# First RMSNorm of a hybrid encoder step: squares added in pairs by DVE, half of them made later on ACT

## The chip, the cores and the metric

The kernel runs on one core of a Trainium2 chip. The metric is the device time of one execution in microseconds. A core has TensorE (PE, with the weight loads shown as PEld), VectorE (DVE), ScalarE (ACT), GpSimd (POOL) and SyncE (SP, which here only issues DMAs), each with its own queue of instructions, run in order. They meet only through semaphores.

## The reference

Two layers of a streaming encoder over 544 tokens (512 of a prompt, 32 of a running stream), model width 1024:

```python
def rmsnorm(x, g):
    x32 = x.astype(jnp.float32)
    y = x32 * lax.rsqrt(jnp.mean(x32 * x32, axis=-1, keepdims=True) + EPS)
    return (y * g.astype(jnp.float32)).astype(x.dtype)

def swiglu(h, wg, wu, wd):
    return (jax.nn.silu(h @ wg) * (h @ wu)) @ wd

# per layer
x = x + 0.5 * swiglu(rmsnorm(x, norm_ffn1), w_gate, w_up, w_down)
x = x + merge(gla(z), band_attention(z)) @ w_out        # z = rmsnorm(x, norm_mix) @ w_in
x = x + 0.5 * swiglu(rmsnorm(x, norm_ffn2), w_gate, w_up, w_down)
# at the end one more rmsnorm
```

There are seven norms. The change concerns the first alone, ahead of layer 0's first FFN.

## The kernel before, in words

**Layout.** Activations lie transposed: `x` is [128 partitions, 8 tiles, 544 tokens], tile k holding features 128k to 128k+127. A norm over features is therefore a sum over partitions and over the eight tiles. The kernel never normalises before a product. It multiplies the weights with x times gain, and scales the products afterwards by S, the inverse root of the mean square of each token. So the sum of squares is wanted only when the first products are there.

**Precision.** Weights and activations are each split into a high part in fp32r (made by ACT, a Copy) and a low part (made by DVE, a subtraction); a product is three fp32r matmuls over 272 tokens, half of the 544.

**Gate and up product.** For each pair of column tiles there is a block of seven products of half size (`a11`, `a12`, `s1`, `s2`, `s4`, `s3`, `a22`), each with four k-tiles, so 84 matmuls a block. They use four PSUM banks; `s2` goes to the bank of `a11`, `s4` to that of `s1`, `s3` again to that of `s2`. TensorE waits (`after_copy` in `block`, L744) until ACT has copied the product that was there (`copy_out`, L1100 to L1104). Block 0 has an order of its own, `FIRST_ORDER`: three k-tiles of `a11`, of `a12` and of `s1`, then the fourth of each, three of `s2`, three of `a22`, the fourth of `s2`, all of `s4` and of `s3`, and the last of `a22`. Between `s3` and that last k-tile of `a22` stands `stats` of the norm.

**Statistics.** `stats(norm)` (L691, its matmul is L700) multiplies a 128x128 matrix of ones with tiles of squares, in plain fp32, once for each half of the tokens, accumulating in PSUM. For all later norms DVE has added the squares up and two tiles are left. For the first norm (`norm == 0`) it takes the eight tiles `first_squares` directly, each when `sq_made` says that it is there. Then ACT takes the square root (`rms_of`, L1033, which needs a table load) and DVE the reciprocal (L1398). Block 1's `s1` on TensorE waits for `rms_ready`, since its bank held the sums.

**Squares of the first norm.** ACT makes them with `first_square(k)` (L1199), into `ev`, `tk`, `tmp`, `sil` and `sq_tmp`, all of them free at this time. The order of ACT's start is written out by hand at L1201 to L1222: splits of tokens and weights as they arrive, squares 0 to 3 between them, then `v_split(0)` (L1060), `t_split(0, 3)` (L1098), `q_split(0)` (L1072), the squares 4 to 7, and then `ffn(0)`. There the function `block` of ACT (L1119) copies `a11`, splits block 1's weights (`x_split`, L1051), copies `s1`, copies `s2`, goes on to `v_split` and `y_split` (L1066) of block 1, the root, the copy of `a22` and `q_split`.

**DVE's start** is written out as well (L1595 to L1615): sums and low parts, ending with `v_split(0)` (L1427), `t_split(0, 3)` (L1474), `q_split(0)` (L1431). Its function `block` (L1506) makes the low part of the next block's weights (`x_split`, L1418), the two adds of `v_sums` (L1440, L1442) and `quads(b, 0)` (L1484), then `v_split`, `y_split` (L1422) and `quads(b, 1)`.

**Loads.** SP issues a raw tile for block b+2 (L490) when DVE has made both the low part and `v_sums` of block b, and its side tile (L498) after `y_split` of block b. POOL adds a second tile to the side tile by an accumulating DMA (L570).

Of the kernel before, what the change touches and what calls it, by code (L numbers as in the profile page):

```python
# [28 lines left out]
ACT = mybir.ActivationFunctionType  # L29
# [10 lines left out]
KT = D_MODEL // P  # L40
# [99 lines left out]
def x_sum(norm, pos):  # L140

    layer, n = divmod(norm - 1, 3)
    return layer * X_SUMS + (DOWN_UNITS - KT, DOWN_UNITS, X_SUMS - KT)[n] + pos + 1
# [46 lines left out]
def encoder_step(nc, xT, bias_rev, vectors,  # L190
# [3 lines left out]
    with ctx:  # L194
        def sb(name, shape, dt=f32, scope=ctx):
            return scope.enter_context(nc.sbuf_tensor(name, shape, dt))

        def sem(name):
            return ctx.enter_context(nc.semaphore(name))


        x = sb("x", [P, KT, T])
# [6 lines left out]
        sq_acc = sb("sq_acc", [P, T])  # L209
        sq_tmp = sb("sq_tmp", [P, T])  # L210
        tmp = sb("tmp", [P, 2, T])
        sil = sb("sil", [P, T])
# [57 lines left out]
        first_squares = [ev[:, 1, n, :] for n in range(2)] + [tk[:, 1, n, :, :].rearrange("p a b -> p (a b)") for n in range(2)]  # L270
# [19 lines left out]
        def block_banks(b):  # L290

            f, i = b // BLOCKS, b % BLOCKS // 2
            return sides(f, sum(i >= i0 for i0, _ in GROUPS) - 1)[b % 2]

        def sums_in(norm):

            layer, n = divmod(norm, 3)
            if n == 1 or norm == 3 * DEPTH:
                return [px[0][:, a, 0:HALF] for a in range(2)]
            return [half[:, 1, 0:HALF] for half in sides(2 * layer + n // 2, 0)[1]]  # L300
# [17 lines left out]

        x_loaded = [sem(f"x_loaded{k}") for k in range(KT)]
        sq_made = sem("sq_made")  # L320
        vec_loaded = sem("vec_loaded")
        ext_loaded = sem("ext_loaded")
        ext_stored = sem("ext_stored")
# [104 lines left out]
        def product(b, p):  # L428

            return len(PRODUCTS) * b + PRODUCTS.index(p) + 1  # L430
# [233 lines left out]
        def _(pe):  # L664
# [26 lines left out]
            def stats(norm):  # L691

                if norm:
                    pe.wait_ge(sq_step, norm * SQ_ADDS)
                squares = [sq_acc[:, :], sil[:, :]] if norm else first_squares
                for a in range(2):
                    for n, sq in enumerate(squares):
                        if a == 0 and sq is not squares[0] or norm == 0:
                            pe.wait_ge(sq_made, KT + norm if norm else n + 1)
                        mm = pe.matmul(sums_in(norm)[a], ones[:, :], sq[:, a * HALF:(a + 1) * HALF],  # L700
                                       start=(n == 0), stop=(n == len(squares) - 1))
                mm.then_inc(stats_done, 1)
# [99 lines left out]
            for layer in range(0, DEPTH):  # L802
# [3 lines left out]
                norm = 3 * layer + 1  # L806
# [210 lines left out]
        def _(act):  # L1017
# [12 lines left out]
            def rms_of(norm):  # L1030
                act.wait_ge(stats_done, norm + 1)
                for a, sums in enumerate(sums_in(norm)):
                    act.activation(S[:, a * HALF:(a + 1) * HALF], sums, ACT.Sqrt, bias=eps[:, :],  # L1033
                                   scale=1.0 / D_MODEL).then_inc(rms_ready, 1)

            def square(norm, n, m):

                act.wait_ge(x_summed, x_sum(norm, n))
                if n >= 3:
                    act.wait_ge(sq_step, (norm - 1) * SQ_ADDS + n - 2)  # L1040
                dst = sq_acc if n == 0 else sil if n % 2 else sq_tmp
                act.activation(dst[:, :], x[:, m, :], ACT.Square).then_inc(sq_made if n == KT - 1 else sq_tile, 1)
# [57 lines left out]
            def copy_out(b, p, dst):  # L1100
                bc, ad = block_banks(b)
                src = {"A": ad[:, 0, 0:HALF], "C": bc[:, 1, 0:HALF], "D": ad[:, 1, 0:HALF]}[BANK[p]]
                act.wait_ge(prod_done, product(b, p))
                act.activation(dst, src, ACT.Copy, scale=-1.0 if p == "s1" else 1.0).then_inc(taken, 1)  # L1104
# [14 lines left out]
            def block(b, begins, after):  # L1119

                part = tk[:, b % 2, :, :, :]
                if b >= 2:
                    act.wait_ge(quad_made, 2 * (b - 2) + 2)
                copy_out(b, "a11", part[:, 0, 0, :])
                if after is not None:
                    x_split(after)
                else:
                    run_split(b, 0)
                copy_out(b, "s1", part[:, 1, 1, :])
                copy_out(b, "s2", part[:, 0, 1, :])  # L1130
                if not begins:
                    block_end(b - 1)
                if after is not None:
                    v_split(after)
                    y_split(after)
                else:
                    run_split(b, 1)
                if b % BLOCKS == 0:
                    rms_of(b // BLOCKS // 2 * 3 + b // BLOCKS % 2 * 2)
                copy_out(b, "a22", part[:, 1, 0, :])  # L1140
                if after is not None:
                    q_split(after)
                else:
                    run_split(b, 2)
                    block_end(b)
# [49 lines left out]

            act.wait_ge(vec_loaded, 16)
            gain = lambda m: g1[:, m:m + 1]
            def first_square(k):
                act.activation(first_squares[k], x[:, k, :], ACT.Square).then_inc(sq_made, 1)  # L1199

            stage(0, 0, gain)  # L1201
            stage(0, 1, gain)
            b_split(0, 0)
# [14 lines left out]
            v_split(0)  # L1218
            t_split(0, 3)
            q_split(0)  # L1220
            for k in range(4, KT):
                first_square(k)  # L1222
            act.wait_ge(const_made, 11)
            for layer in range(0, DEPTH):
                ffn(2 * layer)
# [127 lines left out]
                b = first_block(f, 0)  # L1353
# [28 lines left out]
        def _(dve):  # L1382
# [18 lines left out]
            def square_sum(norm, n):  # L1401
# [3 lines left out]
                    dve.wait_ge(sq_step, (norm - 1) * SQ_ADDS + n - 1)  # L1405
                dve.tensor_tensor(sq_acc[:, :], sq_acc[:, :], (sil if n % 2 else sq_tmp)[:, :], ALU.add).then_inc(sq_step, 1)

            def pair_sums(norm, n):

                if n in (2, 4, 6):  # L1410
                    if n > 2:
                        square_sum(norm, n - 2)
                    square_sum(norm, n - 1)
# [15 lines left out]
            def q_split(b):  # L1429
                dve.wait_ge(q_hi, b + 1)  # L1430
                dve.tensor_tensor(ql[:, :], raw_q[b % 2][:, :], qh[:, :].bitcast(f32), ALU.subtract).then_inc(q_lo, 1)  # L1431

            def v_sums(b):

                n = RAW_POS["block", b]
                raw_there(dve, ("block", b))
                dve.wait_ge(y_summed[b % 2], 16 * (b // 2 + 1))
                if b:
                    dve.wait_ge(v_lo, b)
                dve.tensor_tensor(raw_v[:, 0:SUB], raw_y[b % 2][:, 1, :], raw[n % 2][:, 0:SUB], ALU.add).then_inc(v_part, 1)  # L1440
                dve.wait_ge(v_part, b + 1)
                dve.tensor_tensor(raw_v[:, SUB:2 * SUB], raw_v[:, 0:SUB], raw[n % 2][:, SUB:2 * SUB],  # L1442
                                  ALU.add).then_inc(v_made, 1)
# [33 lines left out]
            def quads(b, half):  # L1477

                bc, ad = block_banks(b)
                part = tk[:, b % 2, half, :, :]  # L1480
                dve.wait_ge(taken, copied(b, "a22" if half else "s2"))
                dve.wait_ge(prod_done, product(b, "a22" if half else "s4"))
                src = ad[:, 0:1, 0:HALF].to_broadcast([P, 2, HALF]) if half else bc[:, :, 0:HALF]
                dve.tensor_tensor(two(ev[:, b % 2, half, :]), part, src, ALU.subtract if half else ALU.add).then_inc(quad_made, 1)  # L1484
# [21 lines left out]
            def block(b, begins, after):  # L1506

                if after is not None:
                    x_split(after)
                else:  # L1510
                    run_split(b, 0)
                if after is not None:
                    v_sums(after)
                quads(b, 0)
                if not begins and b % 2 == 0:
                    hidden_lo(b - 1)
                if after is not None:
                    v_split(after)
                    y_split(after)
                else:  # L1520
                    run_split(b, 1)
                quads(b, 1)
                if after is not None:
                    q_split(after)
                if b % BLOCKS == 0:
                    token_factor(b // BLOCKS // 2 * 3 + b // BLOCKS % 2 * 2)
                block_end(b)
                if after is None:
                    hidden_lo(b)
                    run_split(b, 2)  # L1530
# [82 lines left out]
            v_split(0)  # L1613
            t_split(0, 3)
            q_split(0)  # L1615
            dve.wait_ge(const_made, 11)

            def project(U, slot, dst, columns):
# [5 lines left out]
            for layer in range(0, DEPTH):  # L1624
# [226 lines left out]
                b = first_block(f, 0)  # L1851
# [100 lines left out]
```

## Time and profile before

| | us |
|---|---|
| three runs, median (lowest to highest) | 2110.43 (2108.48 to 2113.02) |
| the profiled execution, its own time | 2113.23 |
| its span, first to last instruction | 2111.3 |
| PE busy in the span | 2061.1 (98%) |
| DVE busy | 1396.4 (66%) |
| ACT busy | 983.5 (47%) |
| POOL busy | 142.1 (7%) |
| mean granted TensorE clock | 0.994 of full |

The span leaves out 1.9 us of the execution's own time. An engine's busy share says how much of the span it worked, not whether it held the others up: that is told by the chain that ended last and by the waits in the timelines. In a timeline row the first number is the start, the second the duration, both in us, "xN" the number of instructions merged, and the bracket the idle time before it with the engine that ended it. Matmuls overlap, so the distance of two starts is what one costs.

### The profile page before, as it was taken

The page shows a single profiled execution, that of the slowest core. Times are in us where ns is not written, and L with a number is a line of the kernel's source. Part 1 is how long each engine was busy: PE and PEld are TensorE (multiplying, and loading weights), DVE is VectorE, ACT ScalarE, POOL GpSimd, SP SyncE. Part 2 cuts the span into 40 slices and gives each one's busy share as a digit, 9 for nine tenths or more (in the row PEclk, how much of TensorE's full clock was granted, in tenths as well). Part 3 has the DMA queues.
Part 4 walks back from the last instruction along what each step waited for, and adds up shares of the span by engine and source line. Part 5 has one row for each costly group of instructions (what it writes and reads, how often), then busy time and mean ns, then how long its engine had stood idle before and what let it go on. Part 6 is the DMA issues. An engine that isn't in the chain of part 4 may idle for free.

```text
span 2111.3 us, 38931 instructions
## 1 busy us (share of the span) xinstructions
PE 2061.1 (98%) x16332; PEld 2011.9 (95%) x16332; DVE 1396.4 (66%) x2019; ACT 983.5 (47%) x1536; POOL 142.1 (7%) x172
## 2 busy tenths in 40 slices
PE   6999999999999999999999999999999999999996
PEld 5999999999889999999999999999988899999996
DVE  6778577635547867668786775864555577685775
ACT  6535255332554635435553543532345555352551
POOL 1100000000110000000000000000020100000001
PEclk9999999999999999999999999999999999999999
DMA  6656463222314556645454654522231236454532
GB/s 183 162 144 162 134 168 104 92 73 75 111 62 120 148 143 168 173 121 165 115 138 132 165 154 114 158 80 84 81 127 62 86 112 163 122 158 130 159 102 73
DMA packets 99453, 265.10 MB, mean 126 GB/s; under 512 B 16336, under 2 KB 16384, under 8 KB 99280
## 3 DMA queue, kind: packets, MB, share of 16 engines
q1 hardware_dynamic: 75152, 200.65, 28.9%
q0 software_dynamic: 24128, 61.97, 15.0%
q8 instruction: 129, 2.11, 0.4%
q14 instruction: 44, 0.36, 0.1%
HBM read 255.28 MB, written 11.44 MB: 126 GB/s over the span
## 4 chain that ended last, share of the span: by engine, by line
PE 96%; DVE 2%; ACT 1%; issue 0%; DMA 0%; SPq 0%; DVEq 0%; ACTq 0%
PE pu L673 30%; PE pu L751 22%; PE px L751 22%; PE px L673 14%; PE px L926 2%; PE px L893 1%; PE px L904 1%; PE pu L700 1%; PE px L798 0%; PE px L864 0%; DMA x<-in_xT 0%; PE px L700 0%; PE px L835 0%; PE px L874 0%; DVE zl L1474 0%
## 5 line engine op out<-in xcount | busy, mean ns | idle before, releaser
L1023 ACT ACTIVATE wh<-raw 128x1024 fp32r<-128x1024 f32 (+1 forms) x116 | 118.0, 1017 | 345.9 <-PE pu L673 227.5
L673 PE MATMUL pu<-zh,wh 128*128 128x272 f32 x1056 | 231.7, 301 | 2.5 <-DVE wl L1387 1.5
L673 PE MATMUL pu<-zh,wl 128*128 128x272 f32 x1056 | 218.7, 289 | 0.0
L673 PE MATMUL pu<-zl,wh 128*128 128x272 f32 x1056 | 218.5, 288 | 0.0
L1387 DVE TENSOR_TENSOR wl<-raw,wh 128x1024 fp32r<-128x1024 f32 (+2 forms) x140 | 163.0, 1165 | 50.3 <-ACT wh L1023 40.7
L673 PEld LDWEIGHTS pu<-zh,wh 128*128 128x128 f32 x1056 | 164.6, 189 | 23.3 <-issue 16.6
L673 PEld LDWEIGHTS pu<-zl,wh 128*128 128x128 f32 x1056 | 166.3, 189 | 0.0
L570 POOL DMA_DIRECT2D raw_y<-in_gate_up x88 | 77.2, 877 | 1319.3 <-DMA raw_y<-in_gate_up 1319.3
L673 PEld LDWEIGHTS pu<-zh,wl 128*128 128x128 f32 x1056 | 165.7, 189 | 0.0
L1418 DVE TENSOR_TENSOR wl<-raw,wh 128x1024 fp32r<-128x1024 f32 x88 | 107.7, 1223 | 57.5 <-ACT wh L1051 57.2
L1051 ACT ACTIVATE wh<-raw 128x1024 fp32r<-128x1024 f32 x88 | 93.3, 1060 | 112.1 <-PE pu L751 39.6
L1104 ACT ACTIVATE tk<-pu 128x272 f32<-128x272 f32 x176 | 69.9, 397 | 123.4 <-PE pu L751 123.4
L1104 ACT ACTIVATE tk<-px 128x272 f32<-128x272 f32 x176 | 69.9, 397 | 122.4 <-PE px L751 122.3
L1066 ACT ACTIVATE yh<-raw_y 128x1024 fp32r<-128x1024 f32 x88 | 93.3, 1061 | 71.1 <-PE px L673 20.5
L673 PE MATMUL px<-hh,wl 128*128 128x272 f32 x600 | 124.2, 288 | 0.0
L673 PE MATMUL px<-hh,wh 128*128 128x272 f32 x600 | 124.0, 288 | 0.0
L673 PE MATMUL px<-hl,wh 128*128 128x272 f32 x600 | 123.7, 288 | 0.0
L751 PE MATMUL px<-zxh,wh 128*128 128x272 f32 x352 | 103.3, 293 | 18.6 <-DVE wl L1418 13.2
L1060 ACT ACTIVATE wh<-raw_v 128x1024 fp32r<-128x1024 f32 x88 | 93.4, 1062 | 59.3 <-PE pu L673 18.1
L1427 DVE TENSOR_TENSOR wl<-raw_v,wh 128x1024 fp32r<-128x1024 f32 x88 | 107.5, 1222 | 14.3 <-ACT wh L1060 14.3
L1422 DVE TENSOR_TENSOR yl<-raw_y,yh 128x1024 fp32r<-128x1024 f32 x88 | 107.5, 1221 | 11.5 <-ACT yh L1066 11.5
L751 PE MATMUL px<-zh,wh 128*128 128x272 f32 x352 | 103.4, 294 | 4.8 <-issue 4.8
(280 smaller groups left out, 6407.1 us busy)
## 6 DMA issues: line engine op xcount, KB each, us to landing
raw<-in_gate_up SPq DMA_DIRECT2D x88, 512.0 KB, 4.2
raw_y<-in_gate_up SPq DMA_DIRECT2D x88, 512.0 KB, 3.9
raw_y<-in_gate_up POOLq DMA_DIRECT2D x88, 512.0 KB, 5.6
raw<-in_down SPq DMA_DIRECT2D x64, 512.0 KB, 3.7
raw<-in_w_in SPq DMA_DIRECT2D x50, 512.0 KB, 3.4
raw_q<-in_gate_up SPq DMA_DIRECT2D x88, 256.0 KB, 3.7
raw<-in_down SPq DMA_DIRECT2D x32, 384.0 KB, 4.2
raw<-in_w_out SPq DMA_DIRECT2D x16, 512.0 KB, 3.5
```

Of the source, the lines that this page charges most:

```text
L570: pool.dma_start(raw_y[b % 2][:, :, :], gate_up[layer, i, mat, 1].rearrange("p (t c) -> p t c", t=2), accum_op=ALU.add).then_inc(y_summed[ ...
L673: mm = pe.matmul(out[:, a, 0:HALF], w[slot][:, k * P:(k + 1) * P], z[:, k, a * HALF:(a + 1) * HALF], start=(first and n == 0), stop=(last ...
L751: mm = pe.matmul(out[BANK[p]], w[:, lhs], z[:, c, kk, :], start=(opens and n == 0), stop=(kk == 3 and n == 2), skip_group_check=True)
L1023: act.activation(unit_hi[slot][0:rows, 0:columns], raw_of(("unit", U))[0:rows, 0:columns], ACT.Copy)\
L1051: act.activation(wh[0][:, :], raw[n % 2][:, :], ACT.Copy).then_inc(x_hi, 1)
L1060: act.activation(wh[1][:, :], raw_v[:, :], ACT.Copy).then_inc(v_hi, 1)
L1066: act.activation(yh[:, :], raw_y[b % 2][:, :, :].rearrange("p t c -> p (t c)"), ACT.Copy).then_inc(y_hi, 1)
L1104: act.activation(dst, src, ACT.Copy, scale=-1.0 if p == "s1" else 1.0).then_inc(taken, 1)
L1387: dve.tensor_tensor(unit_lo[slot][0:rows, 0:columns], raw_of(("unit", U))[0:rows, 0:columns], unit_hi[slot][0:rows, 0:columns].bitcast(f32 ...
L1418: dve.tensor_tensor(wl[0][:, :], raw[n % 2][:, :], wh[0][:, :].bitcast(f32), ALU.subtract).then_inc(x_lo, 1)
L1422: dve.tensor_tensor(yl[:, :], raw_y[b % 2][:, :, :].rearrange("p t c -> p (t c)"), yh[:, :].bitcast(f32), ALU.subtract).then_inc(y_lo, 1)
L1427: dve.tensor_tensor(wl[1][:, :], raw_v[:, :], wh[1][:, :].bitcast(f32), ALU.subtract).then_inc(v_lo, 1)
```

## The change

ACT makes the squares of tiles 4 to 7 not ahead of its first block but inside it, between the copies of `s1` and `s2`. DVE adds the squares two by two, each sum in the place of the first of the two: pairs 0 and 1 behind `q_split(0)`, pairs 2 and 3 in block 0 behind `v_sums(1)` and ahead of `quads(0, 0)`. A new semaphore `sq_paired` counts the sums, and `stats(0)` reads four tiles, each when its sum is there. The later norms stay.

```diff
+        sq_paired = sem("sq_paired")
...
-                squares = [sq_acc[:, :], sil[:, :]] if norm else first_squares
+                squares = [sq_acc[:, :], sil[:, :]] if norm else first_squares[0::2]
                 for a in range(2):
                     for n, sq in enumerate(squares):
                         if a == 0 and sq is not squares[0] or norm == 0:
-                            pe.wait_ge(sq_made, KT + norm if norm else n + 1)
+                            pe.wait_ge(*((sq_made, KT + norm) if norm else (sq_paired, n + 1)))
...
                 copy_out(b, "s1", part[:, 1, 1, :])
+                if b == 0:
+                    for k in range(4, KT):
+                        first_square(k)
                 copy_out(b, "s2", part[:, 0, 1, :])
...
             t_split(0, 3)
             q_split(0)
-            for k in range(4, KT):
-                first_square(k)
             act.wait_ge(const_made, 11)
...
+            def first_pair_sum(j):
+
+                dve.wait_ge(sq_made, 2 * j + 2)
+                dve.tensor_tensor(first_squares[2 * j], first_squares[2 * j], first_squares[2 * j + 1], ALU.add)\
+                    .then_inc(sq_paired, 1)
...
                 if after is not None:
                     v_sums(after)
+                if b == 0:
+                    first_pair_sum(2)
+                    first_pair_sum(3)
                 quads(b, 0)
...
             t_split(0, 3)
             q_split(0)
+            first_pair_sum(0)
+            first_pair_sum(1)
             dve.wait_ge(const_made, 11)
```

`first_square` itself is only moved up in the file, so that `block` can call it.

## Rows read from the trace of the kernel before

**Rows 1.** The page: the span, and the chain that ended last by engine.
```profile
span 2111.3 us, 38931 instructions
...
PE 96%; DVE 2%; ACT 1%; issue 0%; DMA 0%; SPq 0%; DVEq 0%; ACTq 0%
```
**Rows 2.** Windows view of line L700: stretch, length, PE busy, PEld busy, clock, DMA, GB/s.
```profile
36.97:44.28 7.31, 7.31 (x32) 5.89 (x32) 1.00 0.22 77
```
**Rows 3.** Timeline of PE, 23 to 37 us.
```profile
23.39 0.59 PE L751 MATMUL px<-zxh,yh 128*128 128x272 f32 x1 [2.67 <-DVE yl L1422]
...
27.41 0.43 PE L751 MATMUL px<-zxh,yl 128*128 128x272 f32 x1
29.84 0.57 PE L751 MATMUL px<-zh,wh 128*128 128x272 f32 x1 [2.00 <-issue]
30.21 0.43 PE L751 MATMUL px<-zl,wh 128*128 128x272 f32 x1
...
32.70 0.39 PE L751 MATMUL px<-zh,qh 128*128 128x272 f32 x1
32.93 0.29 PE L751 MATMUL px<-zl,qh 128*128 128x272 f32 x1
33.06 0.29 PE L751 MATMUL px<-zh,ql 128*128 128x272 f32 x1
...
36.84 0.29 PE L751 MATMUL px<-zh,yl 128*128 128x272 f32 x1
```
**Rows 4.** Timeline of DVE, 26 to 62 us.
```profile
26.99 1.22 DVE L1427 TENSOR_TENSOR wl<-raw_v,wh 128x1024 fp32r<-128x1024 f32 x1
...
29.33 0.68 DVE L1431 TENSOR_TENSOR ql<-raw_q,qh 128x512 fp32r<-128x512 f32 x1
30.79 1.23 DVE L1418 TENSOR_TENSOR wl<-raw,wh 128x1024 fp32r<-128x1024 f32 x1 [0.79 <-ACT wh L1051]
...
32.65 0.69 DVE L1442 TENSOR_TENSOR raw_v<-raw_v,raw 128x512 f32<-128x512 f32 x1
35.73 0.72 DVE L1484 TENSOR_TENSOR ev<-tk,px 128x544 f32<-128x544 f32 x1 [2.38 <-PE px L751]
...
38.26 1.23 DVE L1422 TENSOR_TENSOR yl<-raw_y,yh 128x1024 fp32r<-128x1024 f32 x1 [0.28 <-ACT yh L1066]
...
61.30 0.68 DVE L1440 TENSOR_TENSOR raw_v<-raw_y,raw 128x512 f32<-128x512 f32 x1
```
**Rows 5.** Timeline of ACT, 26 to 39 us.
```profile
27.18 1.19 ACT L1199 ACTIVATE tmp<-x 128x544 f32<-128x544 f32 x2
28.28 0.64 ACT L1199 ACTIVATE sil<-x 128x544 f32<-128x544 f32 x1
28.82 0.64 ACT L1199 ACTIVATE sq_tmp<-x 128x544 f32<-128x544 f32 x1
29.37 0.37 ACT L1104 ACTIVATE tk<-px 128x272 f32<-128x272 f32 x1
...
30.59 0.38 ACT L1104 ACTIVATE tk<-px 128x272 f32<-128x272 f32 x1
34.14 0.40 ACT L1104 ACTIVATE tk<-px 128x272 f32<-128x272 f32 x1 [3.17 <-PE px L751]
...
38.25 1.28 ACT L1033 ACT_TABLE_LOAD   x1
```
**Rows 6.** DMAs issued from 5 to 12 us: issuer, count, KB, us to landing.
```profile
raw<-in_gate_up SPq DMA_DIRECT2D x1, 512.0 KB, 8.2
...
raw_y<-in_gate_up POOLq DMA_DIRECT2D x1, 512.0 KB, 8.2
```
**Rows 7.** Timeline of POOL around 43 us (the issue of one accumulating load).
```profile
43.44 0.86 POOL L570 DMA_DIRECT2D raw_y<-in_gate_up  x1 [12.21 <-DMA raw_y<-in_gate_up]
```
**Rows 8.** Windows: length, busy of PE, PEld, DVE, ACT, POOL, clock, DMA, GB/s.
```profile
30.00:32.50 2.50, 2.50 (x12) 2.50 (x13) 1.71 (x3) 0.97 (x2) 0.88 (x1) 1.00 0.64 126
33.50:36.00 2.50, 2.50 (x22) 2.50 (x22) 0.27 (x1) 0.74 (x2) 0.00 (x0) 1.00 1.03 238
1725.00:1730.00 5.00, 3.60 (x18) 3.42 (x17) 4.68 (x6) 2.93 (x5) 0.00 (x0) 0.59 0.50 93
```

More of the change, by code:

```diff
@@ L1034, in rms_of, with first_square @@
                                    scale=1.0 / D_MODEL).then_inc(rms_ready, 1)
+            def first_square(k):
+                act.activation(first_squares[k], x[:, k, :], ACT.Square).then_inc(sq_made, 1)
             def square(norm, n, m):
@@ L1197, in _ @@
             gain = lambda m: g1[:, m:m + 1]
-            def first_square(k):
-                act.activation(first_squares[k], x[:, k, :], ACT.Square).then_inc(sq_made, 1)
             stage(0, 0, gain)
```

## The prediction

> **What bounds the kernel now.** The page comes first: TensorE ends the chain for 96% of a span of 2111.3 us [rows 1]. So time is won only where TensorE itself does less or waits less. The sum is made against the profiled execution, 2113.23 us, which lies 2.8 us above the median of the three runs shown, 2110.43, inside 0.1 us of their slowest; I carry the difference over to the median. I count a change under 0.2% (4.2 us) as one that a measurement of this kernel can't tell from none.
>
> Next, the windows view of the statistics line L700 alone. From 36.97 to 44.28 it keeps TensorE busy for the whole of its 7.31 us [rows 2]. That is two halves of the tokens with eight fp32 matmuls each (one per square tile), each matmul recorded as two instructions: 32, one every 229 ns.
>
> Then the timeline of TensorE before it [rows 3]. The third product group (s1) issues its last matmul at 27.41 and the next one, s2, starts at 29.84 after 2.00 us idle. The profile names "issue", not an engine. In the code s2 reuses the bank of a11, so it needs three things: ACT's copy of a11, the low part wl of its weights, and the first token tile. The timelines tell which is last: DVE ends wl at 26.99 + 1.22 = 28.21 [rows 4], ACT ends the a11 copy at 29.37 + 0.37 = 29.74 [rows 5], and TensorE starts 0.10 later. ACT reached that copy late because it made the squares of tiles 4 to 7 ahead of it, 27.18 to 29.37 [rows 5]. So the late copy is what holds TensorE, and the squares hold the copy.
>
> **Part 1: eight matmuls fewer in the statistics.** TensorE now sums four tiles per half, not eight: 8 instructions per half at 229 ns, 16 in all. The price is one half of today's 7.31: 3.66 us less [rows 2]. All of it is on the path, as TensorE has no pause in the stretch. The row that bears on this is the operation itself at the same shape, so no bound is needed but rounding.
>
> **Part 2: four squares moved on ACT.** ACT is free for the a11 copy when qh is done, at 27.18 [rows 5]. a11's last matmul starts six before s1's last, at 27.41 - 6 x 0.226 = 26.05, and at 0.43 us is over by 26.5 [rows 3], so the copy runs 27.18 to 27.55. The last thing s2 waits for is then wl, at 28.21; TensorE starts at about 28.26 instead of 29.84: 1.58 us. The next needs after that: a22 wants ql, ready at 29.33 + 0.68 = 30.01 [rows 4], and TensorE gets there nine matmuls later (28.26 + 9 x 0.226 = 30.3), so nothing is lost; s4 wants the copy of s1.
> On ACT the split of block 1's wh follows at 27.5 (its raw tile, issued before 12 us, takes 8.2 us to land [rows 6]), the s1 copy at 28.5, then four squares of 0.55 each until 31.0. The next copy, s2, waited for TensorE until 34.14 [rows 5] and can't now come before 32.5. The cover is the 3.17 us that ACT idles there; 1.5 us of it stay. Cost nothing.
>
> **Part 3: four adds on DVE.** Price: the add of two 544-column tiles of fp32, 0.72 us at L1484 [rows 4]. The first two stand behind ql: 30.0 to 31.4. Their squares are long made. Behind them are queued the split of block 1's wl (30.79 before, now 31.4), and the two adds of raw_v (over at 33.34 before, now at 33.9). The last two adds follow, 33.9 to 35.3; their squares are there at 31.0. Behind them is queued the quad of block 0 at L1484, which waited for TensorE until 35.73 [rows 4]; with TensorE 1.58 earlier it could run from 34.15, and now runs from 35.3. Who waits for these? ACT's v_split of block 1 wants raw_v, there at 33.9, and had its own wait, s4, until about 34.1. DVE's splits of block 1 end near 38.3 instead of 38.26 + 1.23 = 39.5. TensorE wants the third pair in its statistics 0.9 us, the fourth 1.4 us, after they begin at 35.4: ready at 34.6 and 35.3, needed at 36.3 and 36.8. Cost nothing. If the cover went, each late microsecond of the adds would be one of TensorE's, at most the four of them, 2.9 us; the margins of 1.5 us and more put the value at the other end, zero.
>
> **Part 4: what comes closer behind.** With TensorE 5.2 us earlier, ACT's table load at 38.25, which filled its wait for the statistics, has to be over when they end. It follows y_split, and now runs about 36.6 to 37.9; the statistics end at 39.1. Loads: the SP queue issues block 3's raw tile when the raw_v adds are done, 0.5 us later than before; its side tile follows yl, 1.2 us earlier. The accumulating load behind that one, issued by POOL at 43.44, feeds DVE at 61.30 [rows 4, 7]; an earlier one took 8.2 us to land [rows 6], so over nine us are to spare. After the change it is issued at 42.2 and wanted at 56.1, and nearly six are left. Nothing there.
>
> **The clock.** Rows first: the matmul starts are 0.226 us apart up to 32.93 and 0.127 apart after it [rows 3], the two levels 1.2 and 2.4 GHz for 272 columns (the granted clock is given as 1.00 on both sides [rows 8], so the spacing is what I read). It rose 3.1 us into the stretch that began at 29.84. The stretch before, from s1's first matmul at 23.39 to 27.8, at the same low level [rows 3], and then a pause of 2.0, had not raised it. The change turns that pause into 0.4. A low-clock matmul costs 0.10 more than a fast one, 0.44 us of loss per us at the low level. Three readings: (a) it rises 3.1 us after the stretch begins, now at 31.35: everything moves by 1.58. (b) It rises at the same moment, 32.93: the 1.58 us won are spent at the low level and only 1.58 x 0.56 = 0.9 are left. (c) With the pause nearly gone it rises by 29.5: 5.5 slow matmuls before it and 39.5 at 0.127, so the statistics start at 34.5, 2.4 us earlier, and ql at 30.01 allows little more. I take (a), the middle one.
> The Trainium skill (TensorE: Matmul & The Clock Gate, part 1 on the clock gate) says that the monitor runs free of the kernel, so the moment of the rise differs between runs of one kernel. By that rule neither (a) nor (b) is a law, and the result would lie anywhere from (b) to (c); one execution of before can't show it.
>
> **Sum.** 3.66 + 1.58 = 5.24 us: 2113.23 becomes 2108.0, and on the median 2110.43 - 5.24 = 2105.2.
>
> **Rivals.**
> 1. Clock reading (b): 3.66 + 0.9 = 4.6 us, 2105.8. For it: the rise is not bound to this stretch by anything shown. Chance 0.22.
> 2. Clock reading (c): 3.66 + 2.4 = 6.1 us, 2104.3. For it: a long stretch with a pause of 0.4 looks more like unbroken work. Chance 0.20.
> 3. The moved squares do nothing: another wait ends at 29.8, as the "issue" in the row allows. Then only the matmuls count: 3.66, 2106.8. Against it: the 0.10 us between the copy's end and TensorE's start. The same figure stands if the second and third part bring delays of 1.6 us. Chance 0.10.
> 4. Slower: the low clock lasts. TensorE's start is ragged, and if the rise missed the stretch from 28.26 and didn't come before the end of the first blocks, each us would cost 0.44. From 31.35 on, 12 us more at the low level (a rise at 43) eat the whole gain; a rise at 60 costs 12.6 and gives 2117.8. Against it: it rose within 3.1 us of a steady stretch. Chance 0.04.
> The forecast has 0.44.
>
> **Range and chances.** The cases but the last lie between 2104.3 and 2106.8. On top comes what moves any execution: in the window 1725 to 1730 the granted clock is 0.59 [rows 8], which is 5 x 0.41 = 2 us, far from the change and not bound to repeat; the three runs span 4.5 us. So 2103.0 to 2107.8. Faster by over 0.2% means below 2106.2: four fifths of the forecast, six tenths of rival 1, nine tenths of rival 2 and three tenths of rival 3, together 0.69, put at 0.68. Slower by over 0.2%: 0.03, the last rival. The rest, 0.29, is no difference.
>
> **What would show it.** In the profile of the changed kernel: 16 instructions of L700 around the first norm over 3.66 us; the first s2 matmul at about 28.3, behind wl; the copy of a11 at 27.2; four squares between the copies of s1 and s2; the adds at 0.72 or less with none of them named as TensorE's releaser; the first 84-matmul block 5 us earlier. Wrong would be: s2 still near 29.8, TensorE idle within the statistics, or a wait of blocks 1 to 3 for DVE, ACT or a DMA that is not there now.

## The result, and the profile after

Twelve executions of each kernel give 2108.65 us (2106.21 to 2110.24) against 2112.47 us for the kernel before (2108.48 to 2114.26). The ratio is 0.9985, with a 95% interval of 0.9978 to 0.9992: 3.2 us faster, between 1.7 and 4.6 (the two medians are 3.8 apart; from here on a gain is given by the ratio unless the text says medians). The forecast was 5.24 us less and 2105.2 us. So the sign was right and the size was not: the measured gain lies below the forecast, and the time above the range's upper end of 2107.8. About 2 us of that distance is the base, since the kernel before has its median at 2112.47 over twelve executions and had it at 2110.43 over the first three. The rest is missing gain, 1.4 us by the medians and 2.0 by the ratio.

The profiled execution took 2106.21 us, 7.0 less than the one before. First TensorE in the timeline of the changed kernel (start, duration, what; the bracket is the idle time and who ended it), to be held against [rows 3]:

```profile
28.50 0.60 PE L752 MATMUL px<-zh,wh 128*128 128x272 f32 x1 [1.40 <-DVE wl L1435]
...
31.39 0.43 PE L752 MATMUL px<-zh,qh 128*128 128x272 f32 x1
31.61 0.34 PE L752 MATMUL px<-zl,qh 128*128 128x272 f32 x1
31.80 0.29 PE L752 MATMUL px<-zh,ql 128*128 128x272 f32 x1
...
35.57 0.29 PE L752 MATMUL px<-zh,yl 128*128 128x272 f32 x1
```

The s2 products start at 28.50, not at 29.84, and the wait now ends with DVE's wl, as the forecast had it. TensorE's clock came up at 31.7, 3.2 us into the stretch: there the matmul starts go from 0.227 to 0.127 us apart. The statistics follow at 35.70, in the windows view of their line alone, against the 7.31 us of [rows 2]:

```profile
35.70:39.36 3.66, 3.66 (x16) 2.85 (x16) 1.00 0.32 123
```

ACT's timeline, against [rows 5]: the copy of a11 comes first and the squares later, with 1.66 us of idle time left behind them.

```profile
27.43 0.38 ACT L1108 ACTIVATE tk<-px 128x272 f32<-128x272 f32 x1
...
28.93 1.20 ACT L1038 ACTIVATE tmp<-x 128x544 f32<-128x544 f32 x2
...
30.57 0.65 ACT L1038 ACTIVATE sq_tmp<-x 128x544 f32<-128x544 f32 x1
32.88 0.40 ACT L1108 ACTIVATE tk<-px 128x272 f32<-128x272 f32 x1 [1.66 <-PE px L752]
```

And DVE's, against [rows 4]. The four adds (L1413) end at 35.26, the third and fourth before TensorE asks for them:

```profile
30.17 0.72 DVE L1413 TENSOR_TENSOR ev<-ev 128x544 f32<-128x544 f32 x1
30.80 0.72 DVE L1413 TENSOR_TENSOR tk<-tk 128x544 f32<-128x544 f32 x1
...
34.54 0.72 DVE L1413 TENSOR_TENSOR sil<-sil,sq_tmp 128x544 f32<-128x544 f32 x1
35.17 0.72 DVE L1492 TENSOR_TENSOR ev<-tk,px 128x544 f32<-128x544 f32 x1
```

So up to the statistics everything came nearly as forecast (they begin at 35.70, forecast 35.4). Matching the matmuls of the two traces from their ends, the first one behind the statistics is 4.94 us earlier after the change (5.4 measured from the first matmul, which came 0.48 us later in this execution). Then two differences of 1.5 us each appear at 696 and 1068 us, where the execution before had low-clock stretches that this one had not. And at about 1715 to 1730 and at 1797 the changed kernel loses 0.4 and 0.5 us. At the first of these places the chain of waits of the changed kernel names a load. The chain of the kernel before is TensorE alone there; first a row of `same_as_before`, a second trace of that kernel, then rows of the changed one:

```profile
1683.99 35.37 PE pu L673 x282
```

```profile
1695.66 1.24 DVE wl L1389
1696.90 0.02 issue
1696.91 4.52 DMA raw<-in_gate_up
1701.44 0.02 issue
1701.46 0.70 DVE raw_v L1448
```

The question for the experiments was whether the missing 2 us is chance in the low-clock stretches, a cost of the adds, or something at this place.

### The profile page after: what moved, and what is told of

Same layout as the page of the kernel before. It is cut to its first block, busy times and chain, and to the rows that moved or that the text cites. A ratio compares the mean times of both kernels' runs of the same rounds, so it can differ in the third digit from the quotient of the medians.

```text
span 2104.2 us, 38903 instructions
## 1 busy us (share of the span) xinstructions
PE 2053.6 (98%) x16316; PEld 2004.7 (95%) x16316; DVE 1398.5 (66%) x2023; ACT 983.5 (47%) x1536; POOL 142.0 (7%) x172
## 2 busy tenths in 40 slices
DMA packets 99453, 265.10 MB, mean 126 GB/s; under 512 B 16336, under 2 KB 16384, under 8 KB 99280
## 3 DMA queue, kind: packets, MB, share of 16 engines
q8 instruction: 129, 2.11, 0.4%
## 4 chain that ended last, share of the span: by engine, by line
PE 94%; DVE 3%; ACT 1%; DMA 1%; issue 0%; SPq 0%; DVEq 0%; ACTq 0%
PE pu L674 29%; PE px L752 22%; PE pu L752 22%; PE px L674 14%; PE px L927 2%; PE px L894 1%; PE px L905 1%; PE px L799 0%; PE px L865 0%; DMA raw<-in_down 0%; DVE zl L1482 0%; DVE wl L1389 0%; PE pu L701 0%; PE px L701 0%; PE px L836 0%
## 6 DMA issues: line engine op xcount, KB each, us to landing
raw_q<-in_gate_up SPq DMA_DIRECT2D x88, 256.0 KB, 4.4
```

## The experiments

All medians stand beside executions of the kernel before on the same chip, and each ratio has a 95% interval. It is 3.8 to 5.5 us wide, so the traces have to carry what the medians alone can't.

**Each half alone.** `pairs_only` is the changed kernel with the squares back at their old place:

```diff
                 copy_out(b, "s1", part[:, 1, 1, :])
-                if b == 0:
-                    for k in range(4, KT):
-                        first_square(k)
...
             q_split(0)
+            for k in range(4, KT):
+                first_square(k)
```

> The added pairs and the four tiles in the statistics alone; the squares of tiles 4 to 7 stay ahead of the copy of a11. Theory L (each local gain reaches the end in full, and the shortfall of the whole change is from the low-clock windows that fall elsewhere in an execution): 3.7 us faster than before in the median, give or take the 1 us that such windows move a median; in the profile the first s2 matmul stays at about 29.8 and L701 takes 3.66 us instead of 7.31. Rival P (the adds on DVE push something later and cost time downstream): clearly less than 3.7, about 2, and a wait of TensorE between 45 and 110 us that the kernel before has not.

Measured: 2109.76 against 2111.61 us, ratio 0.9993 (0.9984 to 1.0002), 1.5 us faster. The statistics took 3.66 us, as expected; they began at 38.31, since TensorE's clock stayed at the low level until 35.4 in this execution. Of the 3.66 only 1.5 by the ratio, 1.9 by the medians, arrived, and even the interval's end, 3.4, is short of it. Rival P's number fits, but its sign is missing: the trace keeps its distance to that of the kernel before, matmul by matmul, from the statistics to 450 us.

`move_only` is the kernel before with the move of the squares alone.

> The four squares behind the first copies alone; the statistics sum eight tiles as before. Theory L: the first s2 matmul starts about 1.5 us earlier and the median is 0.9 to 2.4 us faster, by where the clock rises. Rival M (the move is paid back: the clock rises correspondingly later, or another wait takes the place): no gain in the median, 0 plus or minus 0.5, although s2 starts earlier in the profile.

Measured: 2109.63 against 2111.61 us, ratio 0.9992 (0.9983 to 1.0001), 1.7 us faster, within what theory L gave, though the interval just holds rival M's zero too. In its profile the clock was up before s2 already, so the stretch ran as in the third clock reading of the prediction, held for 0.41 us by ql:

```profile
27.81 0.39 PE L751 MATMUL px<-zh,wh 128*128 128x272 f32 x1 [0.77 <-DVE wl L1428]
28.04 0.28 PE L751 MATMUL px<-zl,wh 128*128 128x272 f32 x1
...
29.62 0.40 PE L751 MATMUL px<-zh,qh 128*128 128x272 f32 x1 [0.41 <-DVE ql L1432]
```

The statistics began at 34.26 (36.97 and 37.52 in the two traces of the kernel before), and nothing is lost at 1700 us. So the move does what it promised, and the other half is the one that falls short.

**No change, and more of the disputed work.** `same_as_before` is the kernel before once more; `sums_twice` lets the statistics sum every tile twice:

```diff
-                squares = [sq_acc[:, :], sil[:, :]] if norm else first_squares
+                squares = [sq_acc[:, :], sil[:, :]] if norm else first_squares + first_squares
-                            pe.wait_ge(sq_made, KT + norm if norm else n + 1)
+                            pe.wait_ge(sq_made, KT + norm if norm else min(n + 1, KT))
```

> The kernel before, unchanged. Theory L: ratio 1.000 within about 0.0006, the executions spread over 5 us as in the runs shown; its profile gives a second picture of where the low-clock windows fall, and they fall at other places than 695, 1067, 1490 and 1726 us in part. Rival F (the windows are fixed to the program): the same four places again.

> The kernel before, but the statistics of the first norm sum every tile of squares twice, so 32 instructions more at 229 ns (the mean square of that norm comes out doubled). Theory L: 7.3 us slower than before in the median, local price and price at the end the same. A rival D (part of what changes here is absorbed later, by a stage that has slack for it): clearly less, 4 to 6 us, and the difference between the two traces shrinks at a definite place downstream.

Measured: ratio 1.0004 (0.9995 to 1.0013) for the unchanged kernel, and its low-clock stretches lay at 1065 and 1727 us, none at 695 and 1490. So they aren't fixed, as rival F had it, nor do they fall just anywhere: it is the same few places, and which of them are hit differs between executions. `sums_twice`: 2118.99 against 2111.61 us, ratio 1.0039 (1.0026 to 1.0052). Thirty-two matmul instructions more cost 7.4 us by the medians (8.2 by the ratio, 5.5 to 11), against a local price of 7.3. So 229 ns per instruction is right, and no absorption downstream shows. Taking 16 away brings about half of its price, adding 32 costs all of it. That doesn't look like a matter of a rate, and points to where things fall.

**Adds or statistics.** `four_no_adds` is the kernel before, summing four of its eight tiles, with no adds. `adds_full_sum` is `pairs_only` with each of the four tiles summed twice, so it has the adds and keeps the length of the statistics. The main line of each (the semaphore counts follow it):

```diff
-                squares = [sq_acc[:, :], sil[:, :]] if norm else first_squares
+                squares = [sq_acc[:, :], sil[:, :]] if norm else first_squares[0::2]
...
-                squares = [sq_acc[:, :], sil[:, :]] if norm else first_squares[0::2]
+                squares = [sq_acc[:, :], sil[:, :]] if norm else 2 * first_squares[0::2]
```

> The kernel before, but the statistics of the first norm sum the tiles 0, 2, 4 and 6 only; no adds, DVE's and ACT's instructions as before (half of the squares are left out of the first norm's mean). Theory A (the adds on DVE, or what they shift, cost about 2 us of the 3.7 that the statistics win): the full 3.7 us faster than before, and in its profile no wait for a load of raw near 1700 and 1781 us on the chain. Rival S (the shorter statistics themselves win only about 1.7): 1.5 to 2 us faster, like the kernel with the adds.

> The four adds on DVE as in the changed kernel, squares at their old place on ACT, and the statistics sum each of the four tiles twice, so TensorE has as many instructions as before (the first norm's mean square comes out doubled). Theory A: about 2 us slower than before, with the late loads near 1700 and 1785 us that the two kernels with the adds show. Rival S: no difference from before, within 0.5 us, and no such late loads.

Measured: `four_no_adds` 2109.78 against 2111.50 us, ratio 0.9993 (0.9984 to 1.0002); `adds_full_sum` 2111.93, ratio 1.000 (0.999 to 1.0009). Theory A falls: it wanted the kernel with the adds 2 us slower, where the interval ends at 1.9, and its load lands on time. The shorter statistics without any add win the same 1.5 us as with them. And where theory A had foreseen no late load, without adds, `four_no_adds` shows one. Here are the DMA views of the same load in two kernels, from its issue on for 3.4 us, first `same_as_before`, then `four_no_adds` (queue: packets, MB, share of the engines; then issuer, count, KB, us to landing):

```profile
q1 hardware_dynamic: 144, 0.52, 46.7%
issues: line engine op xcount, KB each, median us to landing
raw<-in_gate_up SPq DMA_DIRECT2D x1, 512.0 KB, 3.4
```

```profile
q1 hardware_dynamic: 137, 0.50, 43.0%
q8 instruction: 1, 0.02, 3.5%
issues: line engine op xcount, KB each, median us to landing
raw<-in_gate_up SPq DMA_DIRECT2D x1, 512.0 KB, 5.0
```

In the second a packet of the instruction queue lies among the load's own. It starts 0.98 us behind the issue, has 16384 bytes and takes 1.89 us, where the load's packets of 4096 bytes take 0.16. The load takes 1.6 us longer to land, and DVE waits for it that much longer, in `same_as_before` and then in `four_no_adds`:

```profile
1708.38 0.69 DVE L1440 TENSOR_TENSOR raw_v<-raw_y,raw 128x512 f32<-128x512 f32 x1 [3.40 <-DMA raw<-in_gate_up]
```

```profile
1706.09 0.69 DVE L1440 TENSOR_TENSOR raw_v<-raw_y,raw 128x512 f32<-128x512 f32 x1 [5.04 <-DMA raw<-in_gate_up]
```

The page counts 129 packets on q8 in the kernels before and after, 2.11 MB. The Trainium skill (Advanced Engine Details and Errata, section on the ISA cache) gives a line of instructions as 16 KB, 256 instructions. The trace agrees: TensorE's 16332 matmuls and as many weight loads, with 538 semaphore records, fill 129.7 such lines, and from one q8 packet to the next TensorE starts 256.0 recorded instructions on average. So q8 carries TensorE's program, and its packets come by the count of TensorE's instructions. The shorter statistics have 16 matmul instructions and their 16 weight loads fewer. With these 32 taken out in front, each later packet comes some 32 instructions later in the work: 16 matmuls at 0.127, 2 us.

`same_as_after` repeats the changed kernel.

> The changed kernel once more, unchanged, on the same chip as the others. Both theories: 3.2 us faster than before, within 1. Theory A expects its profile to show again the chain through the loads of raw near 1697 and 1778 us, at 0.5 us each; if those were chance of one execution they are gone.

Measured: 2107.77 against 2111.50 us, ratio 0.9981 (0.9971 to 0.9990), 4.0 us faster. The load near 1698 was late again, with 4.8 us to landing. The other one, of raw for the down product at 1778 us, was on time here, so that part of the execution shown was not fixed to the kernel.

**A warm TensorE.** `warm_start` puts matmuls of ones, whose result nobody reads, into TensorE's idle times before 28 us:

```diff
+FILL = {("a11", 2): 5, ("s1", 0): 10, ("s2", 0): 6}
...
+            def keep_busy(n):
+
+                for _ in range(n):
+                    pe.matmul(pu[0][:, 0, 0:P], ones[:, :], ones[:, :], start=True, stop=True)
...
+                    if b == 0 and (p, kk) in FILL:
+                        keep_busy(FILL[(p, kk)])
...
+            keep_busy(23)
```

> The changed kernel, with TensorE kept busy in its idle times before 28 us by matmuls of ones whose result nobody reads (23 from the start, then 5, 10 and 6 ahead of the third k-tile of a11, of s1 and of s2). If the clock is up when s2 starts, 45 matmuls run at 0.127 us apart instead of some 13 at 0.226: the statistics start at about 34.8 instead of 35.7, and the median is 1 to 2 us faster than the changed kernel's, 4.5 to 5.5 faster than before. Rival: the fillers don't raise the clock, or they hold the real matmuls up, and it is no faster than the changed kernel.

Measured: 2107.14 against 2111.50 us, ratio 0.9974 (0.9964 to 0.9984), 5.5 us faster. The granted clock was 1.00 from 25 to 35 us, after a fall to the low level at 15.5, and from the start of s2 to the statistics it took 6.4 us instead of 7.2. But s2 itself started later, at 29.14, so the statistics began at 35.59: 0.1 us before those of the changed kernel and not at the 34.8 expected. The warm clock brought nothing that can be seen behind the first block. What this kernel has is its q8 packet 5.5 us behind the issue of the load at 1701 us, out of its way, with 3.3 us to landing. That was not meant, and was the hint for the last three.

**Moving the packets.** `after_pad8` and `four_pad8` give TensorE back the 32 instructions, as eight one-column matmuls in its idle start (each is two matmul instructions and two weight loads). `before_pad56` adds 224 to the kernel before, so that the packets fall where 32 fewer put them, with 56 in the place of 8:

```diff
+            pe.wait_ge(const_made, 1)
+            for _ in range(8):
+                pe.matmul(pu[0][0:1, 0, 0:1], ones[:, 0:1], ones[:, 0:1], start=True, stop=True)
             pe.wait_ge(const_made, 11)
```

> The changed kernel with 8 one-column matmuls of ones in TensorE's idle start, 32 instructions on its queue as the shorter statistics took away, result unread. Theory Q (the 2 us that are missing at the end are lost where a 16 KB packet of the instruction queue q8 falls into the load of raw for block 66, issued near 1701 us: with 32 instructions fewer the packet comes 2 us later and hits that load): the packet is out of the load again, which takes 3.4 us instead of 4.6 to 5.1; TensorE has no stretch of 2.2 us idle near 1719; about 2 us faster than the changed kernel and 5 to 5.5 faster than before. Rival G (the missing part is where the low-clock stretches happen to fall): no difference from the changed kernel, 3.5 us faster than before.

> The kernel that sums the tiles 0, 2, 4 and 6 alone, without adds (half of the squares left out of the first norm), now with the same 8 one-column matmuls at TensorE's start. Theory Q: the full 3.7 us faster than before, against the 1.7 without the 8 matmuls. Rival G: 1.7 again.

> The kernel before with 56 one-column matmuls at TensorE's start, 224 instructions: a 16 KB packet holds 256 of 64 bytes, so that the packets fall where 32 instructions fewer put them. No work of the kernel is changed. Theory Q: the packet hits the load of raw near 1705 us, which takes about 5 us instead of 3.4, TensorE idles 2.2 us instead of 1.5 near 1723, and the kernel is 1.5 to 2 us slower than before. Rival G: no difference from before.

Measured, against 2111.52 us: `after_pad8` 2105.34, ratio 0.9969 (0.9958 to 0.9981), 6.5 us faster; `four_pad8` 2107.70, ratio 0.9984 (0.9975 to 0.9993), 3.4 us faster, nearer to theory Q's 3.7 than to rival G's 1.7, but the interval (1.5 to 5.3) holds both; `before_pad56` 2114.16, ratio 1.0010 (1.0001 to 1.0019), 2.1 us slower with no work changed. In its timeline the 112 instructions of matmul take 2.94 us from 1.05, long over when TensorE's work begins at 14.02. The DMA view of `before_pad56` over the same 3.4 us has the packet, that of `after_pad8` has not:

```profile
q1 hardware_dynamic: 137, 0.50, 45.7%
q8 instruction: 1, 0.02, 3.1%
issues: line engine op xcount, KB each, median us to landing
raw<-in_gate_up SPq DMA_DIRECT2D x1, 512.0 KB, 4.9
```

```profile
q1 hardware_dynamic: 144, 0.52, 48.1%
issues: line engine op xcount, KB each, median us to landing
raw<-in_gate_up SPq DMA_DIRECT2D x1, 512.0 KB, 3.4
```

What TensorE feels of it is its wait for zxl, a low part of the activations that DVE makes later. First `four_no_adds` and `before_pad56`, then `four_pad8` and `after_pad8`, one fence each:

```profile
1721.51 0.39 PE L751 MATMUL px<-zxh,wh 128*128 128x272 f32 x1 [2.19 <-DVE zxl L1469]
```

```profile
1725.48 0.39 PE L751 MATMUL px<-zxh,wh 128*128 128x272 f32 x1 [2.19 <-DVE zxl L1472]
```

```profile
1721.07 0.40 PE L751 MATMUL px<-zxh,wh 128*128 128x272 f32 x1 [1.45 <-DVE zxl L1472]
```

```profile
1717.28 0.39 PE L752 MATMUL px<-zxh,wh 128*128 128x272 f32 x1 [1.45 <-DVE zxl L1480]
```

Of the thirteen traces, the five with the packet in the load (`four_no_adds`, `pairs_only`, both of the changed kernel, `before_pad56`) have 2.19 or 2.20 here, and the eight without it 1.45. There is none in between. In the five the packet starts 0.9 to 2.0 us behind the issue of the load; in seven of the eight it starts 1.0 us or more ahead of the issue and ends before the load's first packets, in `warm_start` it comes after the landing.

The 0.75 us more of idle time isn't all. `four_no_adds` also lost 0.45 us at 1709.6, 12 us earlier, at a wait for the low part wl that DVE makes behind the late load, and its clock stood at the low level for longer. The windows view over 15 us around the place, `same_as_before` and then `four_no_adds` (length, busy of the five engines, granted clock, DMA, GB/s):

```profile
1720.00:1735.00 15.00, 12.15 (x80) 11.62 (x80) 12.35 (x15) 8.67 (x12) 0.86 (x1) 0.89 0.51 141
```

```profile
1716.00:1731.00 15.00, 11.41 (x67) 11.00 (x66) 11.96 (x14) 7.23 (x11) 0.86 (x1) 0.77 0.58 149
```

Eighty matmuls against sixty-seven. Matched matmul by matmul, `four_no_adds` was 3.92 us ahead of `same_as_before` up to this place and 1.47 behind it: 2.4 us given back, half by the waits, half by the clock. `four_pad8` was 3.06 ahead before it and 3.15 at the end.

The clock alone doesn't make the difference. From the matmul that starts at 1700 us in the kernel before to the one at 1745, the five traces with the packet need 45.4 to 46.4 us, mean 45.8, the eight without it 42.4 to 45.0, mean 43.8. Two of the eight (`before`, `after_pad8`) had a low clock for as long as the five and needed 45.0 and 44.9, so at a like clock the packet costs 0.4 to 1.4 us. That the longer waits also bring the low clock more often is likely by these thirteen (all five had it long, two of the eight), but not shown by a run of its own.

## Why the prediction was right or wrong

- **What bounds the kernel**, and the late copy as the reason for the start of s2: right. s2 moved from 29.84 to 28.50 and now waits for wl. Rival 3, that another wait ends at 29.8, is out by these rows; the 1.7 us of `move_only` agree, but its interval alone would not decide.
- **Part 1**, 3.66 us for half of the statistics: right to the digit at its place, and its rate holds at the end (7.4 us by the medians for 32 matmul instructions). But it was written into the sum as if it also arrived in full.
- **Part 2**, 1.58 us: 1.34 by the starts of s2; counted from each execution's first matmul, 1.82. Sound.
- **Part 3**, adds at nothing: no cost was seen. `adds_full_sum` has ratio 1.000 (within 0.001, 2 us), and the adds ran within 0.2 us of the times forecast.
- **Part 4**, "what comes closer behind": here the prediction failed. It looked at the loads of the first blocks for time, and found enough. Its "Nothing there" put all that comes behind at zero. It didn't ask what a shorter instruction stream does to the rest of the program, and the sum took everything behind the statistics as rigid. The local sum stood: behind the statistics the changed kernel was 4.9 to 5.5 us ahead of the two traces of the kernel before. In fact the 32 instructions fewer let a packet of TensorE's instructions fall into a load, issued at 1697 us, that DVE waits for. That costs about 2 us with its share of the clock (45.8 against 43.8 us over the place); with the packet moved away the changed kernel is 6.5 us faster (4.0 to 8.9), which holds the 5.24.
- **The clock**: reading (a) came in the changed kernel, with the rise 3.2 us into the stretch, and (c) in `move_only` and `same_as_after`, where it came before the stretch. Reading (b), the rise at 32.93, came in none. In `pairs_only` it rose 5.2 us into the stretch and in `before_pad56` some 6 us into it, so that the moment isn't tied to the stretch, and the chosen middle was right in the profiled execution by luck. Rival 4, a low clock to 43 us and beyond, didn't come.
- **The range** had no term for the late load, and its centre leaned on three executions whose median lay 2 us below that of twelve. (The profiled execution lay 0.2 us above the slowest of the three, not within 0.1.)

Shown is the chain from the packet to the load, to DVE's wait and to TensorE's, in five traces against eight, and in both directions by instructions that do no work. The medians alone would not do: the intervals of `four_no_adds` and `four_pad8` overlap. Not settled are the 0.5 to 0.9 us that `after`, `pairs_only` and `after_pad8` lose near 1797 us to a late load of raw for the down product. That load takes 8.6 to 9.0 us to land in these three and 5.1 to 6.6 in the other ten. The other kernels lose nothing there, `same_as_after` and `adds_full_sum` among them, which have the adds too. A packet of q8 doesn't decide it: `sums_twice` has one in this load and gets it in 6.4 us, `pairs_only` has none before its last 0.1 us. No run took that load apart.

The lowest ratio is that of `after_pad8`, 0.9969 of the kernel before in six executions. `warm_start` has 0.9974 in nine, and the two intervals overlap.

## What to carry to other kernels

When an edit takes instructions off the engine with the longest stream, or adds some, everything that this engine fetches later shifts, and a load on which another engine waits can be hit far away from the edit. If a gain is whole at its place and half at the end, align the two traces matmul by matmul from the end, find the step, and look at the instruction queue in the DMA view there. A few idle instructions at the start are a cheap way to test it, in both directions.

## What the runs showed of the hardware

- A 16384-byte packet of the instruction queue took 0.9 to 1.9 us around this place and held a 512 KB load back by 1.0 to 1.8 us (3.3 to 3.5 us to landing without it, 4.5 to 5.1 with it), though it is 3% of the load's bytes.
- One-column fp32 matmuls at the start ran at 26 ns for each of their recorded instructions (112 in 2.94 us).
- The same idle times brought TensorE's low clock in one execution and not in another: after idle times of 1.45 and 1.38 us the granted clock was 0.86 over 690 to 702 us in the kernel before, and after 1.45 and 1.40 us it was 1.00 over the same stretch in the changed one. Each such fall cost about 1.5 us (the steps at 696 and 1068 us). Eleven executions of the unchanged kernel spread over 5 us; how much of that is the clock isn't shown.
- Between two packets of TensorE's instruction queue lay 256.0 recorded TensorE instructions on average, 129 packets in 2111 us.
